# Mixture-of-experts weights in a two-block transformer kernel: four consecutive rows (16 KB) per partition, and four chunks taken by TensorE at a time

## What is computed

```python
def ec_moe(h, w_r, w_gate, w_up, w_down):          # 16 experts, d = f = 1024
    cap = max(1, EC_CAPACITY * n // N_EXPERTS)     # 32 tokens per expert
    aff = jax.nn.softmax(jnp.einsum("bnd,de->bne", h, w_r).astype(jnp.float32), axis=-1)
    gates, idx = lax.top_k(jnp.swapaxes(aff, 1, 2), cap)
    xs = h[bidx, idx]
    hid = jax.nn.silu(jnp.einsum("becd,edf->becf", xs, w_gate)) * jnp.einsum("becd,edf->becf", xs, w_up)
    ys = jnp.einsum("becf,efd->becd", hid, w_down) * gates[..., None].astype(h.dtype)
    return jnp.zeros_like(h).at[bidx, idx].add(ys)
```

## Time and profile before

| | us |
|---|---|
| median of 3 runs | 1809.87 |
| lowest and highest run | 1807.76, 1810.55 |
| span of the profiled execution (first to last instruction) | 1797.7 |
| DMA read and written | 561.76 MB, mean 312 GB/s over the span |

### The profile page before, as it was taken

How to read it: one execution, slowest core, us unless ns; L and a number is a source line. 1 busy time by engine, 2 the same in 40 slices (tenths; PEclk the granted TensorE clock), 3 DMA queues, 4 the chain that set the end, 5 groups by cost and what they waited for, 6 DMA issues and landing times.

```text
span 1797.7 us, 18131 instructions
## 1 busy us (share of the span) xinstructions
PE 1329.2 (74%) x7744; PEld 741.4 (41%) x7744; DVE 490.5 (27%) x706; ACT 348.7 (19%) x515; POOL 150.9 (8%) x142
## 2 busy tenths in 40 slices
PE   4988867565587596579775655655556998899999
PEld 1653551121141141169521201212113876779997
DVE  1259450010110000056510100101004644446553
ACT  1111420000010000033300000000003533544442
POOL 1034000000000000010000000000003033440000
PEclk8999969888887798889888988988888988999999
DMA  9898839999999999995479999999999540434530
GB/s 341 355 379 340 322 132 365 409 410 409 404 361 386 406 408 409 407 389 199 152 297 409 410 409 410 410 410 410 410 410 360 208 141 31 159 138 159 187 124 24
DMA packets 160187, 561.76 MB, mean 312 GB/s; under 512 B 9548, under 2 KB 10948, under 8 KB 153470
## 3 DMA queue, kind: packets, MB, share of 16 engines
q1 hardware_dynamic: 155224, 551.83, 78.7%
q0 software_dynamic: 2208, 8.36, 1.2%
q10 hardware_dynamic: 2694, 0.68, 0.2%
HBM read 557.69 MB, written 3.16 MB: 312 GB/s over the span
## 4 chain that ended last, share of the span: by engine, by line
PE 33%; DMA 28%; SPq 4%; DVE 3%; ACT 2%; issue 1%; POOL 0%; DVEq 0%; ACTq 0%; POOLq 0%
PE ps L1821 21%; DMA ring<-in_moe_w_down 12%; DMA ring<-in_moe_w_up 12%; SPq L457 4%; DMA ring<-in_moe_w_gate 4%; PE ps L2062 4%; PE ps L1806 3%; PE ps L2070 1%; DMA ring<-in_w_in 1%; PE ps L2267 0%; PE ps L2095 0%; PE ps L2255 0%; PE ps L2257 0%; PE ps L1868 0%; ACT ring_parts L579 0%
## 5 line engine op out<-in xcount | busy, mean ns | idle before, releaser
L2062 PE MATMUL ps<-ring,scratch 128*32 128x512 f32 x3072 | 472.6, 753 | 321.8 <-DMA ring<-in_moe_w_up 134.8
L2062 PEld LDWEIGHTS ps<-ring,scratch 128*32 128x32 f32 x3072 | 97.2, 124 | 671.3 <-DMA ring<-in_moe_w_up 205.7
L1821 PE MATMUL ps<-ring_parts,scratch_parts 128*128 128x512 f32 x656 | 185.3, 401 | 5.1 <-DVE scratch_parts L1353 1.4
L1821 PE MATMUL ps<-scratch_parts,ring_parts 128*128 128x256 f32 x704 | 146.0, 282 | 0.0
L1821 PEld LDWEIGHTS ps<-ring_parts,scratch_parts 128*128 128x128 f32 x656 | 122.3, 188 | 35.7 <-issue 5.0
L579 ACT ACTIVATE ring_parts<-ring 128x2048 fp32r<-128x2048 f32 x56 | 106.1, 1920 | 93.7 <-PE ps L1821 87.4
L1821 PEld LDWEIGHTS ps<-scratch_parts,ring_parts 128*128 128x128 f32 x704 | 116.2, 191 | 0.3
L423 DVE TENSOR_TENSOR ring_parts<-ring,ring_parts 128x2048 fp32r<-128x2048 f32 x44 | 100.7, 2289 | 53.4 <-ACT ring_parts L579 52.1
L1431 DVE TENSOR_TENSOR scratch<-ps,gate_bc 128x512 f32<-128x512 f32 x16 | 10.3, 686 | 306.5 <-PE ps L2062 306.5
L1423 DVE TENSOR_TENSOR scratch<-scratch,ps 128x1024 f32<-128x1024 f32 x8 | 9.8, 1221 | 298.0 <-PE ps L2062 298.0
L1821 PE MATMUL ps<-xT_parts,ring_parts 128*128 128x256 f32 x288 | 80.9, 281 | 1.3 <-DVE xT_parts L1130 1.3
(11 more groups left out here) (375 smaller groups left out, 1584.0 us busy)
## 6 DMA issues: line engine op xcount, KB each, us to landing
ring<-in_moe_w_gate SPq DMA_DIRECT2D x64, 2048.0 KB, 23.4
ring<-in_moe_w_up SPq DMA_DIRECT2D x64, 2048.0 KB, 23.7
ring<-in_moe_w_down SPq DMA_DIRECT2D x64, 2048.0 KB, 23.9
ring<-in_ada_w SPq DMA_DIRECT2D x24, 2048.0 KB, 12.2
ring<-in_mlp_w SPq DMA_DIRECT2D x16, 2048.0 KB, 8.5
ring<-in_sc_w_in SPq DMA_DIRECT2D x6, 2048.0 KB, 21.0
ring<-in_w_in SPq DMA_DIRECT2D x6, 2048.0 KB, 18.0
ring<-in_xattn_wkv SPq DMA_DIRECT2D x4, 2048.0 KB, 24.4
```

The source lines that it names most:

```text
L1821: last = mm(out, lhs[x], rhs[y], start=start and n == 0, stop=stop and n == 2)
L2062: last = mm(ps[32 * j:32 * j + 32, banks[half], :], src[:, k, CAP * j:CAP * (j + 1)], w[:, j, 512 * half:512 * half + 512], start=(k == 0) ...
```

## The change

**What a chunk is.** The rows are counted anew. With `RUN = 4`, a step of 512 rows of the model dimension is split so that partition p has the four consecutive rows 4 p to 4 p + 3 of it. A chunk is now one expert's step: 128 partitions with 16 KB each, contiguous in DRAM. Four chunks (the four experts) make a step, two steps make a product; the number of chunks and their bytes stay.

**How it is taken.** `product` waits for the four chunks of a step, does the same 32 matrix products in the same order as before, and the last of them raises `chunks_used` by 4.

**What follows from the new row order.** Whatever is transposed or gathered into the layout of the contraction takes every fourth column (`run_slice`: stride of 16 bytes in SBUF): the transposes of the normed rows for the two mixtures, the gather, the transposes of the hidden rows, and the shift and scale columns of those norms. The router's weights are loaded in the same order, four rows of 64 bytes together. The gain of the norm has its own load (`grow2`) and four small transposes at the start.

```diff
+RUN = 4
+STEPS = KD // RUN
...
+        def run_order(v):
+            return v.rearrange("p (k i j) -> p k j i", i=P, j=RUN)
+        def run_slice(v, k):
+            return run_order(v)[:, k // RUN, k % RUN, :]
...
-                gate = a["moe_w_gate"][l].rearrange("(g e) (k p) f -> g k p e f", e=EG, k=KD)
+                gate = a["moe_w_gate"][l].rearrange("(g q e) (k p j) f -> g k q p e (j f)", g=GROUPS, q=RUN, p=P, j=RUN)
...
-                        sp.dma_start(slot4(base + c), w[g, k])\
+                        sp.dma_start(ring[:, slot_of(base + c), :].rearrange("p (e f) -> p e f", e=EG // RUN), w[g, k // RUN, k % RUN])\
                             .then_inc(sem(f"slot{(base + c) % SLOTS}_loaded"), 16)
...
+            sp.dma_start(grow2, a["norm2_g"].rearrange("l (k c) -> (l k) c", k=STEPS)).then_inc(sem("gains_in"), 16)
...
-                act.dma_start(wr[:, l], a["moe_w_r"][l].rearrange("(k p) e -> p k e", k=KD)).then_inc(sem("params_in"), 16)
+                act.dma_start(wr[:, l].rearrange("p (k j) e -> p k j e", j=RUN), a["moe_w_r"][l].rearrange("(k p j) e -> p k j e", p=P, j=RUN)).then_inc(sem("params_in"), 16)
...
+                        cols = run_slice(src[:, t, :], k) if name in ("moe0", "moe1") else src[:, t, P * k:P * (k + 1)]
...
-            nc.tensor.transpose(ps[:, 1, 0:GAINS], grow[0:GAINS, :], ident[0:GAINS, 0:GAINS]).then_inc(sem("gains_ps"), 1)
+            nc.tensor.transpose(ps[:, 1, 0:GAINS], grow[0:GAINS, :], ident[0:GAINS, 0:GAINS])
+            for j in range(RUN):
+                last = nc.tensor.transpose(ps[:, 1, GAINS:GAINS + 2 * KD].rearrange("p (r j) -> p j r", j=RUN)[:, j, :],
+                                           grow2.rearrange("r (i j) -> r j i", j=RUN)[:, j, :],
+                                           ident[0:2 * STEPS, 0:2 * STEPS])
+            last.then_inc(sem("gains_ps"), 1)
...
-                        for k in range(KD):
-                            w = chunk(c0 + k)
-                            if second and k == KD // 2:
-                                pe.wait_ge(sem(second), n + 1)
-                            for half in range(2):
-                                for j in range(EG):
-                                    last = mm(ps[32 * j:32 * j + 32, banks[half], :], src[:, k, CAP * j:CAP * (j + 1)],
-                                              w[:, j, 512 * half:512 * half + 512], start=(k == 0), stop=(k == KD - 1))
-                            used(last)
+                        for step in range(STEPS):
+                            w = [chunk(c0 + RUN * step + q) for q in range(RUN)]
+                            for k in range(RUN * step, RUN * step + RUN):
+                                if second and k == KD // 2:
+                                    pe.wait_ge(sem(second), n + 1)
+                                for half in range(2):
+                                    for j in range(EG):
+                                        col = F * (k % RUN) + 512 * half
+                                        last = mm(ps[32 * j:32 * j + 32, banks[half], :], src[:, k, CAP * j:CAP * (j + 1)],
+                                                  w[j * RUN // EG][:, j % (EG // RUN), col:col + 512],
+                                                  start=(k == 0), stop=(k == KD - 1))
+                            last.then_inc(sem("chunks_used"), RUN)
...
-                            last = mm(ps[:, 6 + k // 4, P * (k % 4):P * (k % 4 + 1)], rows[:, t, P * k:P * (k + 1)],
+                            last = mm(ps[:, 6 + k // 4, P * (k % 4):P * (k % 4 + 1)], run_slice(rows[:, t, :], k),
...
-                        last = nc.tensor.transpose(ps[:, 6 + k // 4, P * (k % 4):P * (k % 4 + 1)], hid[:, P * k:P * (k + 1)],
-                                                   ident)
+                        last = nc.tensor.transpose(ps[:, 6 + k // 4, P * (k % 4):P * (k % 4 + 1)], run_slice(hid, k), ident)
```

More of the change, by code:

```diff
@@ L188, in build @@
         crow = at(9464, i=P)
+        grow2 = gate_bc[0:2 * STEPS, 0:P * RUN]
         ada_b = at(9984, i=512)
@@ L338, in build @@
         SCALE = {"x": 0, "ctx": 1, "moe0": 2, "mix1": 3, "moe1": 4}
-        GAIN = {"mix2": 4, "mem": 5, "xattn": 6, "mlp": 7}
+        GAIN = {"mix2": 2, "mem": 3, "xattn": 4, "mlp": 5}
         def affine(name):
@@ L364, in build @@
         SC_SPLITS = EV_SPLITS + 16
-        GAINS = (8 + SCK) * KD
-        cw1 = gcol[:, 8:8 + SCK, :].rearrange("p j c -> p c j")
+        GAINS = (6 + SCK) * KD
+        NORM2 = 6 + SCK
+        cw1 = gcol[:, 6:6 + SCK, :].rearrange("p j c -> p c j")
         PARAMS = 10
@@ L449, in experts @@
                 l, g0, g1, base = loop
-                gate = a["moe_w_gate"][l].rearrange("(g e) (k p) f -> g k p e f", e=EG, k=KD)
-                up = a["moe_w_up"][l].rearrange("(g e) (k p) f -> g k p e f", e=EG, k=KD)
-                down = a["moe_w_down"][l].rearrange("(g e) (k p) d -> g k p e d", e=EG, p=P)
+                gate = a["moe_w_gate"][l].rearrange("(g q e) (k p j) f -> g k q p e (j f)", g=GROUPS, q=RUN, p=P, j=RUN)
+                up = a["moe_w_up"][l].rearrange("(g q e) (k p j) f -> g k q p e (j f)", g=GROUPS, q=RUN, p=P, j=RUN)
+                down = a["moe_w_down"][l].rearrange("(g q e) (k p j) d -> g k q p e (j d)", g=GROUPS, q=RUN, p=P, j=RUN)
                 with sp.Fori(g0, g1) as g:
@@ L464, in _ @@
             first = 0
-            for g in (a["norm1_g"], a["norm2_g"], a["norm_mix_g_2"].unsqueeze(0), a["norm_mem_g_2"].unsqueeze(0),
+            for g in (a["norm1_g"], a["norm_mix_g_2"].unsqueeze(0), a["norm_mem_g_2"].unsqueeze(0),
                       a["norm_xattn_g_2"].unsqueeze(0), a["norm_mlp_g_2"].unsqueeze(0), a["sc_conv_w"][0]):
@@ L1173, in mod_cols @@
                 else:
-                    last = scale(("moe0", "moe1")[g // 3], 0, 2 + g // 3)
+                    last = scale(("moe0", "moe1")[g // 3], 0, NORM2 + g // 3)
                 last.then_inc(sem("mod_cols"), 1)
@@ L1206, in _ @@
             dve.wait_ge(sem("gains_ps"), 1)
-            nc.vector.tensor_copy(flat(gcol[:, :, :]), ps[:, 1, 0:GAINS]).then_inc(sem("gain_cols"), 1)
+            nc.vector.tensor_copy(flat(gcol[:, :, :]), ps[:, 1, 0:GAINS + 2 * KD]).then_inc(sem("gain_cols"), 1)
             normed("x", h, rows)
@@ L1782, in ada_columns @@
                 for b in range(4):
-                    last = nc.tensor.transpose(ps[:, bank, P * b:P * (b + 1)], mrow[:, g % 3, b, :], ident)
+                    src = run_slice(flat(mrow[:, g % 3]), b) if g % 3 else mrow[:, g % 3, b, :]
+                    last = nc.tensor.transpose(ps[:, bank, P * b:P * (b + 1)], src, ident)
                 last.then_inc(sem("mod_T"), 1)
```

4 lines of the change are left out of this document (2 added, 2 removed).

## The result

The changed kernel takes 1819.68 us (median of 19 runs, 1806.11 to 1824.3), the kernel before 1807.67 us beside it (19 runs, 1794.69 to 1812.41). The ratio is 1.0074, with an interval of 1.0054 to 1.0094: +13.4 us (the medians are 12.0 us apart). The time lies inside the range that was given, but the forecast was -1.4 us, too little to be told from no change, and a small loss is what came.

A forecast was written before the change was run, and what follows sets the result against it. The prediction took the expert weights' DMAs to set the pace of four stretches, A to D; 40.0 us gained, 47.5 lost and 8.9 absorbed made -1.4 us, so 1808.5 us, range 1796 to 1829.

The forecast's parts named there:

- 5, strided reads: Gather and transposes read their stationary operand at a stride of 16 bytes: +1 us taken, between 0 and +11.
- 1, pace: Expert weights' DMAs: 16 KB pieces save 0.25 us a chunk on 160 streaming chunks, -40 us.
- 2, first release: Start of each of four expert stretches: first ring slots freed only with the fourth chunk, +5.2 us each, +20.8.
- C's part: Third expert stretch: TensorE could be 6.6 us later at no cost, so -6.6 us of the first-release loss.
- 3, behind the last landing: End of each stretch: four chunks remain after the last DMA lands, a 9.5 us burst, +25.7 us in all.
- The rivals that had bursts at one clock only: TensorE bursts all at 2.4 GHz, 7.0 us (1798.5 us, chance 0.20), or all at 1.2 GHz, 14.2 us (1827, 0.12).
- 4, steady state: Middle of the stretches: slots are released early enough that the DMAs never pause, so no cost.
- 6, the start: Kernel start: four tiny transposes and an 8 KB load more, off the path, so no cost.
- The end of D: Second block's norm after the last expert stretch: up to 3.2 us earlier, -2.3 us as TensorE's transposes then bind.
- the stride binds: Rival: strided loads set the pace of gather and transposes, +10 us on the sum, 1819 us, chance 0.14.

The follow-up runs named there:

- e3: Kernel before, with only the gather and both sets of transposes reading at a stride of 16 bytes; 1815.55 us, ratio 1.0051.
- e1: Kernel before, with only the 16 KB pieces of the change, chunks still taken one by one; 1772.08 us, ratio 0.9786.
- e9: e4 with the first eight gate chunks of each stretch loaded in 4 KB pieces and taken one by one; 1790.24 us, ratio 0.9912.
- e2: Kernel before, 4 KB pieces and old layout, but TensorE waits for four chunks and releases four; 1849.96 us, ratio 1.0249.
- e4: Changed kernel, but VectorE writes the normed rows in TensorE's reading order, so gather and norm transposes read contiguously; 1814.24 us, ratio 1.0041.
- e10: e9 with the last four down chunks of each stretch also loaded in 4 KB pieces and taken one by one; 1781.44 us, ratio 0.9854.

## Why the prediction was wrong, point by point

It missed by 13.4 us in the trace (+12.0 against -1.4; that this is also the figure of the ratio is chance). By its own steps:

- **5, strided reads: the step that failed.** +1 was taken, with +11 as the upper bound and a rival of 0.14. Measured: +8.9 in the four gathers; +9.2 us for the whole kernel in e3. For the gathers the working of the bound was right to the decimal (0.24 us a product, +3.8 in C). The choice between the ends was not: "the load has half of its time covered" took the overlap of two loads of 228 ns for slack, and in the gather there was none, since the interval from one MATMUL to the next doubled. It was 0.24 us at a granted clock of 0.71 as of 1.00, so the clock doesn't hide it. For the transposes the bound's 2 us didn't come: at the full clock 8 of them went from 1.07 to 1.20 us ahead of D's routing and from 1.09 to 1.24 in the groups, though their loads took 212 ns instead of 141. The Trainium skill (SBUF — State Buffer, Door 1: The DMA port swizzle, the note on "cachelines") has lines of 16 bytes that want two hits each. By that rule, the gather's rows agree: the reads with a line to themselves (stride of 16 bytes) took twice the time, those with two a line (8 bytes) 0.2 us more, 7.70 and 4.01 us against 3.81. The transposes' rows don't: either stride costs them the same, 1.24 and 1.23 us against 1.09.
- **1, pace: right in kind, 5 us too large, the second term that missed.** Forecast -40; measured -34.6 in the changed kernel's trace, -36.0 in that of e1, -38.7 us as e1's time. The forecast went on from 8 KB with 0.07 to 0.11 us less a chunk and took 4.87 us, 431 GB/s; 16 KB came at 428. D gave 19.8 for its 88 chunks, 0.225 each and not 0.25; the bursts there are 4.9 us a chunk apart. B gave 3.7 of 4.0, A 9.0 of 10.0, C 2.0 of 4.0. The alternative of the Trainium skill (DMA: Bandwidth & Descriptors, Why small descriptors are slow), 3 cycles a packet and 14 us in all, is measured wrong for these lengths: it is less than half of the gain.
- **2, first release: right.** +20.8 forecast, 5.15 a stretch and +20.6 measured. C's part was -6.6, and came at -7.9; but e9 shows that it is not tied to this step.
- **3, behind the last landing: right.** Bursts of 8.9 to 9.9 us where 9.5 was taken, +26.1 where +25.7 was. The rivals that had bursts at one clock only (7.0 or 14.2) fall.
- **4, steady state: right.** 428 GB/s within D, 409 in e2.
- **6, the start:** nothing of it is seen; A's gather starts at times between 258 and 265 us in the traces of all kernels.
- **The end of D: right for one event, failed for the next.** -2.3 forecast, -0.8 measured. The squares of the norm did come 3.2 us earlier: 4.1 us behind VectorE's first scaling of rows (1380.65 - 1376.56) instead of 7.3 (1376.35 - 1369.06). ScalarE's two splits no longer waited for the `in_w_in` chunk but for TensorE's last burst, and behind them the squares waited 0.32 us more for `h`. What was late next was GpSimd, which works out the norm's factor from the squares, and not TensorE's transposes. ScalarE and GpSimd in the changed kernel, then GpSimd before:

```profile
1376.62 3.71 ACT L594 ACTIVATE ring_parts<-ring 128x2048 fp32r<-128x2048 f32 x2 [8.63 <-PE ps L2086]
1380.65 1.06 ACT L564 ACTIVATE xT<-h 128x1024 f32<-128x1024 f32 x1 [0.32 <-DVE h L1452]
...
1381.87 0.54 POOL L1056 DMA_DIRECT2D small<-in_xattn_q_norm_g  x1
1382.48 1.16 POOL L989 TENSOR_SCALAR ms<-ss 128x1 f32<-128x1 f32 x1
1383.72 1.43 POOL L990 TENSOR_TENSOR rstd<-ms,mhalf 128x1 f32<-128x1 f32 x1
1385.24 0.75 POOL L989 TENSOR_SCALAR ms<-ss 128x1 f32<-128x1 f32 x1
1386.07 0.54 POOL L990 TENSOR_TENSOR rstd<-ms,mhalf 128x1 f32<-128x1 f32 x1
```

```profile
1377.58 0.18 POOL L974 TENSOR_SCALAR ms<-ss 128x1 f32<-128x1 f32 x1 [2.68 <-ACT xT L549]
1377.85 0.56 POOL L975 TENSOR_TENSOR rstd<-ms,mhalf 128x1 f32<-128x1 f32 x1
1378.62 0.63 POOL L974 TENSOR_SCALAR ms<-ss 128x1 f32<-128x1 f32 x1 [0.21 <-ACT xT L549]
1379.33 0.54 POOL L975 TENSOR_TENSOR rstd<-ms,mhalf 128x1 f32<-128x1 f32 x1
```

  Before, GpSimd had waited 2.68 us for the squares. Now it was issuing DMAs until 1382.4, and its first two operations lasted 1.16 and 1.43 us instead of 0.18 and 0.56 (its times are rough). Its last one ended 10.0 us behind the scaling instead of 10.8: of the 3.2 us, 0.8 were left.
- **Outside the sum:** 1.4 us more between C and D, 1.7 less between A and B. The 1.4 are not the stride's: e4 has 1.7 and e1 2.5 us more there, and their transposes of the normed rows read contiguous words. The cause of both is open.

Together: strides 7.9 (the gathers' 8.9 less the 1.0 taken), pace 5.4, the end of D 1.5, C to D 1.4, work behind the last landings 0.4, less 1.3 in C, 0.2 of release and 1.7 between A and B: 13.4. The rival "the stride binds", 1819, is the case that came, with a chance of 0.14. That its time met the measured one so closely is luck in part: the pace fell 5.4 us short, and of the stride's +11 us 8.9 came. It deserved a larger chance: two rows (the load's length, and the product's interval of half of it) pointed to loads that set the gather's pace, and no row spoke for cover.

What stays open: that the short chunks at the ends in e10 cost 0.4 us each and not 0.2, why the strides cost the gather and not the transposes, and why the second block has two lengths.

## What to carry to other kernels

Longer DMA pieces and the taking by several that they force are two changes: the first pays on every chunk that streams, the second costs a few times a stretch, at its first release and behind its last landing. Ask whether the coarse form is needed at the ends, since a chunk with the same rows in another shape can give the fine form there (with contiguous rows, that took the ratio from 1.0041 in e4 to 0.9854 in e10, from +7 to -26 us). And an operand that is newly strided is to be priced by the operand's own load, at its bound, wherever rows suggest that these loads set the pace; one experiment with the stride alone settles it (e3).

## What the chip showed that was not expected

- The gather's stationary fp32 operand of 128 x 128 read at a stride of 16 bytes: 0.24 us a MATMUL, at a granted clock of 0.71 as of 1.00. At a stride of 8 bytes: 4.01 us for 32 MATMULs where contiguous ones take 3.81. Transposes with such an operand: 1.24 and 1.23 us for eight, where contiguous ones take 1.09.
- The DMAs' rate goes on rising from 8 to 16 KB pieces, but by less than before: 410, 422 and 428 GB/s for 4, 8 and 16 KB.
- The two lengths of the second block lie in the clock of its first part. Windows of before (short), then of e4_rows_permuted (long):

```profile
1500.00:1550.00 50.00, 48.41 (x236) 37.84 (x237) 22.43 (x41) 20.20 (x41) 12.22 (x6) 1.00 0.35 127
```

```profile
1500.00:1550.00 50.00, 50.00 (x180) 37.31 (x180) 15.76 (x34) 11.80 (x27) 8.03 (x4) 0.69 0.20 73
```

  In the first the clock is back at 2.4 GHz throughout, in the second it is at 1.2 GHz for most of it, with TensorE busy all the time; 180 MATMULs instead of 236. The times of the kernel before fall into both lengths (1795 to 1801 and 1807 to 1812 us), so there it differs from one execution to the next. Those of e4_rows_permuted (12 runs, 1812.5 to 1817.5) show one length only, which suggests that the kernel has a part in it; the cause is open.
